# Output projection's first rows read ahead, and attention's first operands loaded during compression

## The chip, the cores and the metric

The kernel runs on one core of a Trainium2 chip. The time is that of the device, in microseconds, from one launch; lower is better. The core has TensorE (matmuls and transposes, into the accumulators of PSUM), VectorE, ScalarE, GpSimd and SyncE, each with an instruction stream of its own; they meet at semaphores. Transfers between memory (HBM) and on-chip tiles go through 16 DMA engines and are issued by SyncE and GpSimd.

## The reference, cut to what matters

One transformer layer for 2048 tokens of width 1024, in float32.

```python
h = rmsnorm(x, g_mix_pre);  z = h @ w_in          # queries, keys, values, gates of 16 heads' worth
o_a = nsa_mixer(...)       # 6 heads: gates * (compressed + selected + window of 512)
o_b = dilated_mixer(...)   # 4 heads, each over three pairs (window, dilation)
o_c = banded_attention(..., sinks=...)            # 6 heads, window of 128
mix = jnp.concatenate([o_a, o_b, o_c], axis=-1) @ w_out
x = x + rmsnorm(mix, g_mix_post)
f = conv_glu_ffn(rmsnorm(x, g_ffn_pre), w_up, conv_w, conv_b, w_down)
x = x + rmsnorm(f, g_ffn_post)
```

Compression turns windows of 32 keys (and values) of the nsa heads into one each: `gelu(flat @ w1 + b1) @ w2`. The compressed attention also chooses the 8 blocks that the selected attention reads.

## The kernel before, in words

Five blocks run one after the other, and a block begins when every engine has finished the one before: `project`, `compress`, `attend`, `mix_out` and `ffn`. Precision is kept by splitting operands into an upper part (rounded) and a lower part (the rest) and using three matmuls.

**project** normalises 16 tiles of 128 rows, turns them, and keeps them on the chip as `h_hi` and `h_lo` (8 rows of blocks c by 2048 tokens). VectorE makes `h_lo` at L410, one operation for each of the 16 tiles. Then 33 blocks of columns of w_in are multiplied (L526) and stored as `z_hi` and `z_lo` in memory. In the last block (L516) the first five rows c are done for all tokens, so that the tiles of rows 0 and 1 come free: SyncE then loads the windows (`x_raw`, over `h_hi`) and first weights (`w1_raw`, over `h_lo`) of the next block into them.

**compress** takes these operands, splits them and multiplies (L650). SyncE issues the second half of the weights, small tables and the overlap table, and waits for the latter.

**attend** has 30 units: a unit is one kind of attention of one head (k: compressed; b: one dilated pair; c: window of 128; w: window of 512; s: selected), of 16 tiles of 128 queries. The order is k, b, b six times, then c six times, then w, s six times. For a tile n TensorE makes scores (L1248, L1249) into one of three PSUM buffers, VectorE adds the bias and finds the lowest (L1437), ScalarE takes the exponential (L1358), TensorE turns the weights (L1260), VectorE or ScalarE copies them (L1344), and once four tiles are turned TensorE multiplies the values (L1285), ScalarE copies the sum (L1366), TensorE turns it back (L1298) and VectorE finishes it (L1461 to L1494). All four engines run one loop over steps n; light tiles have six weight buffers (`w_small`), wide ones three (`w_big`), and scores are issued so many tiles ahead, in the first unit in blocks: tiles 0 to 5 at step 0, 6 to 9 at step 4 (weighed at step 5), 10 to 13 at step 8. Ahead of this loop ScalarE waits for the gates and takes their exponential (L1350), and VectorE prepares the sinks, waits for ScalarE and finishes the gates (L1401 to L1405). TensorE waits ahead of it for the identity matrix. SyncE issues the first loads in this order: identity, queries of unit 0, its table, sinks, gates, queries of unit 1, keys 0, table, values 0, keys 1, values 1. Later loads follow as a unit is scored, biased or summed. The queries lie in `low[:, 0:2]`, the second slot of keys in `low[:, 2:4]`. The last unit of all, the selected attention of head 5, takes its groups of four tiles in falling order (`falling`, `at`), heavy ones first, and uses the wide buffers only. At its end SyncE stores the head and waits for all stores to land.

**mix_out** (the output projection) loads the attention rows of a tile of 128 tokens (L1643 to L1645), turns them (L1809), ScalarE rounds them (L1726) and VectorE makes the lower part (L1763), TensorE multiplies with `w_out` (L1827). The weights were loaded in attention's last units; here ScalarE rounds eight rows of them (L1711), GpSimd and VectorE make the lower parts of four rows each (L1695). VectorE does two of its rows before tile 0's lower part, two after.

**ffn** follows and is not touched but for the place of one scratch tile.

Of the kernel before, what the change touches and what calls it, by code (L numbers as in the profile page):

```python
# [6 lines left out]
F32 = mybir.dt.float32  # L7
F32R = mybir.dt.float32r
# [48 lines left out]
MOVES = tuple(range(6, 22))  # L57

# [14 lines left out]
def project(nc, x, g_pre, ident, w_z, w_ffn, pos_t, z_hi, z_lo, z_pair, v_heads, gates, f_hi, f_lo, w1, w1_copy, w_out, wo_copy, wo_moved,  # L73
# [4 lines left out]
    with ExitStack() as ctx:  # L78
# [5 lines left out]
        idt = sb("idt", [P, P])  # L84
# [83 lines left out]

        def last_of(j):

            return 7 + j if j < 2 else 4 * j + 4

        @blk.sync
        def _(sp):
# [32 lines left out]
            for j in range(2, NZ):  # L207
# [168 lines left out]
        def _(dve):  # L376
# [27 lines left out]
            for t in range(NT):  # L404
                if t >= 6 and t % 2 == 0:
# [4 lines left out]
                dve.tensor_tensor(h_lo[:, :, cols], turned_tile(t % 2), h_hi[:, :, cols].bitcast(F32),  # L410
                                  ALU.subtract).then_inc(hlo_done, 1)
# [36 lines left out]
        def _(pe):  # L448
# [14 lines left out]
            def project_early(i, half):  # L463
# [7 lines left out]
                for c in range(4 * half, 4 * half + 4):  # L471
                    for q, (w, h) in enumerate(((w_hi, h_hi), (w_lo, h_hi), (w_hi, h_lo))):
                        last = pe.matmul(banks[:, bank, :], w[:, j, c, :], h[:, c, tok],
# [31 lines left out]
            for j in range(2, NZ):  # L505
# [4 lines left out]
                for c in range(rows):  # L510
                    for n in range(4):
                        if c == 0:
                            pe.wait_ge(zhi_done, 4 * (j - 2) + n + 1)
                        tok = slice(n * 512, (n + 1) * 512)
                        for q, (w, h) in enumerate(((w_hi, h_hi), (w_lo, h_hi), (w_hi, h_lo))):
                            last = pe.matmul(banks[:, 4 * k + n, :], w[:, k, c, :], h[:, c, tok],  # L516
                                             start=(c == 0 and q == 0), stop=False)
                    last.then_inc(last_row, 1)
                for n in range(4):
# [4 lines left out]
                    for c in range(rows, DC):  # L524
                        for q, (w, h) in enumerate(((w_hi, h_hi), (w_lo, h_hi), (w_hi, h_lo))):
                            last = pe.matmul(banks[:, 4 * k + n, :], w[:, k, c, :], h[:, c, tok],  # L526
                                             start=(c == 0 and q == 0), stop=(c == DC - 1 and q == 2))
# [18 lines left out]
def compress(nc, z_pair, w1_copy, b1_t, w2, overlap, x_raw, w_raw, w_hi, poss, x_in, w_in, pos_in, last_out, kc_hi, kc_lo, vk):  # L546
# [4 lines left out]
    with ExitStack() as ctx:  # L551
# [13 lines left out]
        over_in = sem("over_in")  # L565
        zeroed = sem("zeroed")
# [33 lines left out]
        def _(sp):  # L600
# [5 lines left out]

            sp.wait_ge(zeroed, 3)
# [3 lines left out]
            sp.wait_ge(last_out, 8 * 16)  # L611

        @blk.gpsimd
        def _(pool):
# [10 lines left out]
            pool.memset(vk[0:NC, :, HD:HD + 1], 1.0).then_inc(ones_done, 1)  # L625

# [101 lines left out]
class Unit:  # L728


    def __init__(self, kind, h, fold, back, q_row, k_row, v_head, falling=False):
# [5 lines left out]
        self.at = [4 * (NT // 4 - 1 - t // 4) + t % 4 if falling else t for t in range(NT)]  # L737
        for t in self.at:
# [29 lines left out]
def attention_units():  # L768
# [11 lines left out]
    for h in range(6):  # L780
        units.append(Unit("w", h, 1, 4, h * HD, 13 * P + h // R * HD, 2 + h // R))
        units.append(Unit("s", h, 1, NT - 1, h * HD, 12 * P + h // R * HD, h // R, falling=(h == 5)))
# [30 lines left out]
def attend(nc, ident, z_hi, z_lo, v_heads, gates, bias_b, bias_c, bias_s, bias_w, own_block, sinks, cmp_bias, pick_bias,  # L813
           kc_hi, kc_lo, vk, sel_t, parts, near_parts, o_heads, o_mid, q2, k_hi, k_lo, near, w_small, qm, vs,
           wo_copy, wo_moved, w_rows, w_in):
# [14 lines left out]
    out_at = Slots(heads, lambda u, n: n % 2)  # L830

# [8 lines left out]
    for n in range(N):  # L840
# [6 lines left out]
        mine, size = (narrow, SMALL) if len(unit.tiles[t]) * P <= NARROW and u < NU - 1 else (wide, BIG)  # L847
# [79 lines left out]
    with ExitStack() as ctx:  # L927
        sb, ps, sem = scope(nc, ctx, "a_")
        idt = sb("idt", [P, P])
# [1358 lines left out]
```

## Time and profile before

| | us |
|---|---|
| median of 3 runs | 3513.67 |
| lowest, highest | 3513.1, 3516.63 |
| the profiled execution: its own time | 3511.8 |
| its span, first to last instruction | 3510.0 |
| TensorE busy in it | 3395.0 (97%) |
| VectorE busy | 1387.6 (40%) |
| ScalarE busy | 1161.3 (33%) |
| GpSimd busy | 569.2 (16%) |

In profile rows PE is TensorE's matmuls, PEld its weight loads (beside the matmuls), DVE VectorE, ACT ScalarE, POOL GpSimd, SPq SyncE's queue of issues. "L12" is a line of the kernel. In brackets behind a row stand the idle time of the engine just before and what ended it. The span's mean granted clock of TensorE was 0.989 of full speed. The blocks begin at about 796.5 (compress), 830.7 (attend), 1811.2 (mix_out) and about 2051.2 us (ffn).

### The profile page before, as it was taken

Reading aid. Unit: us, or ns where it says so; the run is one execution under the profiler, and the core shown is the slowest. Engines: PE = TensorE matmul, PEld = TensorE weight load, DVE = VectorE, ACT = ScalarE, POOL = GpSimd, SP = SyncE. Lnnn points to the kernel's source line nnn. Section 1 sums busy time; section 2 is a strip of 40 time slices with the busy share of each in tenths; the row PEclk is TensorE's granted clock in tenths of the full one; section 3 lists DMA queues with packets and bytes.
Section 4 is the critical chain, followed back from the end, with each engine's and each line's share of the span. In section 5 each row is a group of like instructions: output and inputs, shape, how many; then the busy total and the mean of one; then the engine's idle time right before and its main releaser. Section 6 shows DMA issues by size and latency. Waiting matters only on the chain. (4 is left out here: it accounts for less than half of the span.)

```text
span 3510.0 us, 45328 instructions
## 1 busy us (share of the span) xinstructions
PE 3395.0 (97%) x16530; PEld 2708.8 (77%) x16530; DVE 1387.6 (40%) x3825; ACT 1161.3 (33%) x1979; POOL 569.2 (16%) x503
## 2 busy tenths in 40 slices
PE   8999999997998999999989999999999999999998
PEld 6888888886777866666658878887888788888886
DVE  5111101105766766666645444403441244115421
ACT  5111111115665755555433333302330133113310
POOL 1556654430000013232010000000000000000000
PEclk9999999998999999999999999999999999999999
DMA  5789965657888732232036775566556655665553
GB/s 190 265 304 320 320 242 197 213 186 178 205 196 205 174 91 63 77 93 55 28 106 206 234 276 192 192 239 224 192 192 239 232 192 191 239 227 203 191 192 143
DMA packets 299524, 676.15 MB, mean 193 GB/s; under 512 B 99408, under 2 KB 155216, under 8 KB 285136
## 3 DMA queue, kind: packets, MB, share of 16 engines
q1 hardware_dynamic: 265616, 517.93, 45.9%
q0 software_dynamic: 33696, 155.40, 12.3%
q8 instruction: 133, 2.18, 0.3%
q14 instruction: 79, 0.65, 0.1%
HBM read 496.06 MB, written 185.57 MB: 194 GB/s over the span
## 5 line engine op out<-in xcount | busy, mean ns | idle before, releaser
L1285 PE MATMUL a_ot_ps<-a_turned_w,vs 128*65 128x128 f32 (+3 forms) x1452 | 448.6, 420 | 1.2 <-issue 1.2
L526 PE MATMUL z_banks<-h_hi,z_w_hi 128*128 128x512 f32 x972 | 387.3, 398 | 0.0
L526 PE MATMUL z_banks<-h_lo,z_w_hi 128*128 128x512 f32 x972 | 384.5, 396 | 0.0
L526 PE MATMUL z_banks<-h_hi,z_w_lo 128*128 128x512 f32 x972 | 384.4, 395 | 0.0
L1563 PE MATMUL banks<-low,f_own 128*128 128x512 f32 x1344 | 323.7, 401 | 12.4 <-issue 6.3
L1563 PEld LDWEIGHTS banks<-low,f_own 128*128 128x128 f32 x1344 | 258.0, 192 | 73.9 <-issue 13.6
L1358 ACT ACTIVATE w_small<-w_small,a_negm 128x128 f32<-128x128 f32 (+3 forms) x505 | 244.1, 517 | 160.6 <-DVE a_negm L1437 97.1
L1285 PEld LDWEIGHTS a_ot_ps<-a_turned_w,vs 128*65 128x65 f32 x1452 | 179.3, 139 | 81.3 <-issue 68.5
L1437 DVE CUSTOM_DVE_ANT_0 w_small<-a_s_ps,near 128x128 f32<-128x128 f32 (+2 forms) x456 | 169.1, 393 | 168.2 <-PE a_s_ps L1249 141.5
L526 PEld LDWEIGHTS z_banks<-h_lo,z_w_hi 128*128 128x128 f32 x972 | 182.6, 188 | 44.1
L526 PEld LDWEIGHTS z_banks<-h_hi,z_w_lo 128*128 128x128 f32 x972 | 182.8, 188 | 42.7
L526 PEld LDWEIGHTS z_banks<-h_hi,z_w_hi 128*128 128x128 f32 x972 | 182.8, 188 | 42.4
L310 ACT ACTIVATE st_hi<-z_banks 128x512 fp32r<-128x512 f32 (+1 forms) x100 | 59.7, 597 | 462.2 <-PE z_banks L526 331.6
L1260 PE MATMUL a_t_ps<-a_idt,w_small 128*128 128x128 f32 x1077 | 210.0, 277 | 0.0
L445 DVE TENSOR_TENSOR st_lo<-z_banks,st_hi 128x512 fp32r<-128x512 f32 x76 | 52.3, 691 | 396.8 <-ACT st_hi L310 318.0
L1344 ACT ACTIVATE a_turned_w<-a_t_ps 128x512 f32<-128x512 f32 (+3 forms) x255 | 138.7, 548 | 208.0 <-PE a_t_ps L1260 207.1
L2101 DVE SCALAR_TENSOR_TENSOR f_acc<-banks,vk,f_gp 128x1024 f32<-128x1024 f32 x16 | 20.5, 1284 | 454.3 <-POOL vk L1933 454.3
L1248 PE MATMUL a_s_ps<-low 128*128 128x512 f32 (+3 forms) x384 | 186.7, 489 | 2.5 <-DMA low<-z_lo 1.5
L2041 ACT ACTIVATE f_u<-banks 128x512 f32<-128x512 f32 x176 | 105.0, 596 | 237.6 <-PE banks L1563 237.5
L1563 PE MATMUL banks<-low,k_hi 128*128 128x512 f32 x768 | 179.6, 390 | 0.0
L1563 PE MATMUL banks<-low,k_lo 128*128 128x512 f32 x768 | 179.3, 389 | 0.0
L2078 DVE COPY f_u<-f_halo 128x2 f32<-128x2 f32 x176 | 29.7, 169 | 368.7 <-ACT f_u L2041 355.2
(239 smaller groups left out, 6533.2 us busy)
## 6 DMA issues: line engine op xcount, KB each, us to landing
f_own<-f_hi SPq DMA_DIRECT2D x88, 512.0 KB, 3.6
f_own<-f_lo SPq DMA_DIRECT2D x88, 512.0 KB, 4.5
z_xs<-in_w_ffn POOLq DMA_DIRECT2D x33, 1024.0 KB, 8.2
f_hi<-z_v_hi POOLq DMA_DIRECT2D x33, 1024.0 KB, 4.9
f_lo<-z_xs POOLq DMA_DIRECT2D x33, 1024.0 KB, 5.6
low<-z_hi SPq DMA_DIRECT2D x48, 512.0 KB, 7.7
k_hi<-f_hi SPq DMA_DIRECT2D x44, 512.0 KB, 3.6
k_hi<-f_lo SPq DMA_DIRECT2D x44, 512.0 KB, 4.5
```

The lines of the kernel that those rows point to most:

```text
L310: act.activation(out.bitcast(F32) if is_value(j) else out, bank, ACT.Copy).then_inc(zhi_done, 1)
L445: dve.tensor_tensor(low, bank, high, ALU.subtract).then_inc(zlo_done, 1)
L526: last = pe.matmul(banks[:, 4 * k + n, :], w[:, k, c, :], h[:, c, tok], start=(c == 0 and q == 0), stop=(c == DC - 1 and q == 2))
L1248: pe.matmul(out, query, hi[:, start + a:start + z], start=True, stop=False)
L1260: ins = pe.transpose(t_ps[:, b % TB, i, :], weights(n)[:, x * P:(x + 1) * P], idt[:])
L1285: last = pe.matmul(ot_ps[0:out_width(g), at:at + count * P], values, rows, start=(x == 0), stop=(x == len(blocks) - 1), skip_group_check=True)
L1344: ins = eng.activation(out, src, ACT.Copy) if e == 0 else eng.tensor_copy(out, src)
L1358: act.activation(weights(n), weights(n), ACT.Exp, bias=negm[:, n % 32:n % 32 + 1], scale=-1.0)\
L1437: dve.tensor_tensor_reduce(weights(n)[:, a:z], s_ps[:, c % SB, 0:z - a], table[:, at + a:at + z], -0.125, floor, ALU.add, ALU.min, low).th ...
L1563: last = pe.matmul(out, w[:, c * P:(c + 1) * P], rows[:, c, :], start=(c == 0 and x == 0), stop=(c == DC - 1 and x == 2))
L2041: act.activation(u[:, k, b, 2:QT + 2], banks[:, 2 * k + b, :], ACT.Copy).then_inc(u_done, 1)
L2078: dve.tensor_copy(u[:, k, b, 0:2], halo[:, b, j, :]).then_inc(edge_done, 1)
```

## The change

- Compression's SyncE also loads, between its small tables and the overlap table: the queries of units 0 and 1 (`low` rows 0 and 1), the two tables of these units, and the keys of unit 2 (`low` rows 2 and 3). GpSimd's zeroing of the lower half of `low[:, 3]` moves there too. For this `low` and `near` are allocated from the start, and `low` is also the first half of `h_lo` in project, whose other half is the new tile `h_lo2`; the last block's order of rows is `LAST_ROWS`, and the loads of project's end wait for rows 1, 3 and 4 of it.
- Attention's SyncE begins with the keys and values of unit 1 and the values of unit 2, then sinks and gates. TensorE waits for no identity (it stays from project), ScalarE takes the gates' exponential at step 6, VectorE does sinks and gates at the end of step 7.
- The last unit runs in rising order and may use the small buffers. When its first half is finished, SyncE stores that half, and then loads the rows of tiles 0 and 1 of the output projection into the free query slot (`first_o`). The second half's store is no longer waited for in attention (semaphore `o_last`), but in the projection, ahead of the loads of tiles 2 and 3.
- The projection's ScalarE rounds two rows of weights ahead of tile 0, not four, and VectorE makes tile 0's lower part before all its weights.

```diff
+LAST_ROWS = (0, 4, 5, 1, 2, 3, 6, 7)
...
-                    sp.wait_ge(last_row, 2)
+                    sp.wait_ge(last_row, 1)
                     load_windows(sp, z_pair, x_raw, x2_in, 0)
+                    sp.wait_ge(last_row, 3)
                     load_first(sp, w1_copy, w1_raw, w1_in, 0)
+                    sp.wait_ge(last_row, 4)
                     load_windows(sp, z_pair, x_raw, x2_in, 1)
...
-                dve.tensor_tensor(h_lo[:, :, cols], turned_tile(t % 2), h_hi[:, :, cols].bitcast(F32),
-                                  ALU.subtract).then_inc(hlo_done, 1)
+                for part, tile in enumerate(h_lo):
+                    rows = slice(4 * part, 4 * part + 4)
+                    last = dve.tensor_tensor(tile[:, :, cols], turned_tile(t % 2)[:, rows], h_hi[:, rows, cols].bitcast(F32),
+                                             ALU.subtract)
+                last.then_inc(hlo_done, 1)
...
+            first = attention_units()[:3]
+            for s, unit in enumerate(first[:2]):
+                rows = slice(unit.q_row, unit.q_row + HD)
+                sp.dma_start(low[0:HD, s, :].bitcast(F32), z_hi[rows, :]).then_inc(units_in, 16)
+                sp.dma_start(low[HD:P, s, :].bitcast(F32), z_lo[rows, :]).then_inc(units_in, 16)
+            sp.dma_start(near[:, 0, 0:CW], cmp_bias[0]).then_inc(units_in, 16)
+            sp.dma_start(near[:, 1, 0:2 * P], bias_b[0]).then_inc(units_in, 16)
+            rows = slice(first[2].k_row, first[2].k_row + HD)
+            for half in range(2):
+                sp.dma_start(low[half * HD:(half + 1) * HD, 2, :].bitcast(F32), z_hi[rows, :]).then_inc(units_in, 16)
+            sp.dma_start(low[0:HD, 3, :].bitcast(F32), z_lo[rows, :]).then_inc(units_in, 16)
...
+            sp.wait_ge(units_in, 16 * 9)
...
+            pool.memset(low[HD:P, 3, :].bitcast(F32), 0.0).then_inc(ones_done, 1)
...
-        self.at = [4 * (NT // 4 - 1 - t // 4) + t % 4 if falling else t for t in range(NT)]
...
-        mine, size = (narrow, SMALL) if len(unit.tiles[t]) * P <= NARROW and u < NU - 1 else (wide, BIG)
+        mine, size = (narrow, SMALL) if len(unit.tiles[t]) * P <= NARROW else (wide, BIG)
...
+                if u == NU - 1:
+                    sp.dma_start(o_heads[unit.h, :, NT // 2:], oh[:, s, NT // 2:, 0:HD]).then_inc(o_last, 16)
...
-            sp.dma_start(idt[:], ident).then_inc(id_in, 16)
-            load_q(0, 0)
-            load_near(0, 0)
+            load_k(0, 1)
+            load_v(0, 1)
+            load_v(1, 2)
             sp.dma_start(sink[:], sinks.partition_broadcast(P)).then_inc(sink_in, 16)
             sp.dma_start(gate[:], gates).then_inc(gate_in, 16)
-            load_q(1, 1)
-            load_k(0, 1)
-            load_near(1, 1)
-            load_v(0, 1)
-            load_k(1, 2)
-            load_v(1, 2)
+            def load_ahead(u):
+
+                s, h = out_at.slot[out_at.of_unit[u]], units[u].h
+                sp.wait_ge(out_done, 4 * u + 2)
+                sp.dma_start(o_heads[h, :, 0:NT // 2], oh[:, s, 0:NT // 2, 0:HD]).then_inc(stored[s], 16)
+                for e in range(2):
+                    sp.wait_ge(stored[e], out_seen[e])
+                    sp.wait_ge(ob_out[e], 16)
+                sp.wait_ge(scored, through(NU - 3))
+                for t in range(2):
+                    pair = first_o[:, t, :].rearrange("p (h d) -> p h d", d=HD)
+                    sp.dma_start(pair[:, 0:6], heads_in[:, 0:6, t * HD:(t + 1) * HD]).then_inc(ahead_in, 16)
+                    sp.dma_start(first_o[:, t, 384:640], o_mid[t * P:(t + 1) * P, :]).then_inc(ahead_in, 16)
+                    sp.dma_start(pair[:, 10:16], heads_in[:, 6:12, t * HD:(t + 1) * HD]).then_inc(ahead_in, 16)
...
-            for s in range(2):
-                sp.wait_ge(stored[s], out_seen[s])
+            sp.wait_ge(ahead_in, 16 * 6)
...
-            act.wait_ge(gate_in, 16)
-            act.activation(gate[:], gate[:], ACT.Exp, scale=-1.0).then_inc(gexp_done, 1)
-            act.wait_ge(sink_done, 1)
...
             for n in range(N + 6):
+                if n == 6:
+                    act.wait_ge(gate_in, 16)
+                    act.activation(gate[:], gate[:], ACT.Exp, scale=-1.0).then_inc(gexp_done, 1)
...
+                if n == 7:
+                    gates_and_sinks()
...
-            for k in range(2):
-                load_o(k, k)
...
+            sp.wait_ge(o_last, 16)
+            for k in range(2):
+                load_o(2 + k, k)
...
-            for c in range(4):
+            for c in range(2):
                 upper(c)
...
-            split_lower(dve, 1, 0, 4)
             take_o(0, 0)
-            split_lower(dve, 1, 4, DC)
+            split_lower(dve, 1, 0, DC)
...
+                rows = first_o if isinstance(t, int) and t < 2 else ot
```

## Rows read from the trace of the kernel before

**Rows 1.** Waits of TensorE over the span: total us, times, longest

```profile
PE z_banks L459 <- DVE z_xs L391: 16.1, 4, 9.9
...
PE banks L1809 <- DMA p_ot<-o_heads: 11.9, 1, 11.9
PE a_s_ps L1248 <- DMA low<-z_lo: 10.8, 2, 9.2
```

**Rows 2.** Timeline around attention's start: start us, us, engine, line, operation

```profile
829.14 0.29 DVE L724 COPY vk<-c_vc_ps 127x128 f32<-127x128 f32 x1 [0.17 <-PE c_vc_ps L663]
...
830.68 1.28 ACT L1350 ACT_TABLE_LOAD   x1 [2.16 <-PEq L551]
...
838.97 0.44 ACT L1350 ACTIVATE a_gate<-a_gate 128x288 f32<-128x288 f32 x1 [7.00 <-DMA a_gate<-gates]
...
841.77 0.29 DVE L1437 CUSTOM_DVE_ANT_0 w_small<-a_s_ps,near 128x128 f32<-128x128 f32 x1
...
842.17 2.27 ACT L1358 ACTIVATE w_small<-w_small,a_negm 128x128 f32<-128x128 f32 x6 [2.76 <-DVE a_negm L1437]
...
845.01 0.29 DVE L1437 CUSTOM_DVE_ANT_0 w_small<-a_s_ps,near 128x128 f32<-128x128 f32 x1 [1.00 <-PE a_s_ps L1249]
...
845.34 1.68 ACT L1358 ACTIVATE w_small<-w_small,a_negm 128x128 f32<-128x128 f32 x4 [0.17 <-DVE a_negm L1437]
...
848.65 0.28 DVE L1437 CUSTOM_DVE_ANT_0 w_small<-a_s_ps,near 128x128 f32<-128x128 f32 x1
...
851.41 0.29 DVE L1437 CUSTOM_DVE_ANT_0 w_small<-a_s_ps,near 128x128 f32<-128x128 f32 x1
```

**Rows 3.** Timeline of SyncE's issues at attention's start

```profile
833.29 0.43 SPq L1080 DMA_DIRECT2D a_gate<-gates  x1
...
836.18 0.60 SPq L1048 DMA_DIRECT2D k_lo<-z_lo  x1
...
837.45 0.53 SPq L1051 DMA_DIRECT2D vs<-v_heads  x1
```

**Rows 4.** DMA issues of these three moments: count, KB each, us to landing

```profile
a_gate<-gates SPq DMA_DIRECT2D x1, 144.0 KB, 5.7
...
k_lo<-z_lo SPq DMA_DIRECT2D x1, 512.0 KB, 14.9
...
vs<-v_heads SPq DMA_DIRECT2D x1, 520.0 KB, 15.3
```

**Rows 5.** Busy us by engine in compression's later part; then clock, DMA share, GB/s

```profile
808.50:829.00 20.50, 20.50 (x165) 20.05 (x163) 8.62 (x11) 6.79 (x10) 0.00 (x0) 1.00 0.01 2
```

**Rows 6.** The same (PE, PEld, DVE, ACT, POOL) for two stretches of attention's start

```profile
842.10:847.10 5.00, 4.97 (x21) 4.54 (x22) 2.49 (x18) 4.39 (x11) 0.00 (x0) 0.50 1.03 218
848.60:851.40 2.80, 2.43 (x18) 1.85 (x18) 2.20 (x14) 1.61 (x5) 0.00 (x0) 1.00 0.96 231
```

**Rows 7.** Timeline from attention's end into the output projection

```profile
1805.54 0.57 SPq L1074 DMA_DIRECT2D o_heads<-a_oh  x1
...
1815.76 1.94 PE L1809 MATMUL banks<-p_idt,p_ot 128*128 128x128 f32 x8 [11.94 <-DMA p_ot<-o_heads]
...
1821.91 0.78 PE L1827 MATMUL banks<-p_w_hi,p_oh 128*128 128x512 f32 x1
...
1833.86 1.04 PE L1809 MATMUL banks<-p_idt,p_ot 128*128 128x128 f32 x8
```

**Rows 8.** Timeline of VectorE there: first and last of its four weight rows

```profile
1813.22 2.53 DVE L1695 TENSOR_TENSOR p_w_lo<-k_hi,p_w_hi 128x1024 fp32r<-128x1024 f32 x1 [1.93 <-ACT p_w_hi L1711]
...
1823.16 3.42 DVE L1695 TENSOR_TENSOR p_w_lo<-near,p_w_hi 128x1024 fp32r<-128x1024 f32 x1
```

**Rows 9.** Busy us in attention's last two pairs of units, columns as in rows 5

```profile
1619.30:1715.50 96.20, 95.19 (x514) 64.19 (x511) 61.84 (x217) 48.78 (x71) 13.51 (x18) 1.00 0.13 34
1715.50:1803.80 88.30, 85.77 (x453) 56.40 (x450) 51.46 (x170) 41.14 (x56) 4.80 (x7) 1.00 0.15 54
```

**Rows 10.** VectorE's groups by form, first 75 us: count, busy us, mean ns, idle before

```profile
L410 DVE TENSOR_TENSOR h_lo<-z_banks,h_hi 128x1024 fp32r<-128x1024 f32 x16 | 19.5, 1221 | 9.1 <-ACT h_hi L281 9.1
```

More of the change, by code:

```diff
@@ L167, in early @@
             return 4 + i % 4, i % 4, i % 2, i // 2
+        hi_rows, lo_rows = [h_hi[:, c] for c in range(DC)], [h_lo[c // 4][:, c % 4] for c in range(DC)]
         def last_of(j):
@@ L509, in _ @@
                 rows = 5 if j == NZ - 1 else 0
-                for c in range(rows):
+                order = LAST_ROWS if rows else tuple(range(DC))
+                for c in order[:rows]:
                     for n in range(4):
-                        if c == 0:
+                        if c == order[0]:
                             pe.wait_ge(zhi_done, 4 * (j - 2) + n + 1)
                         tok = slice(n * 512, (n + 1) * 512)
-                        for q, (w, h) in enumerate(((w_hi, h_hi), (w_lo, h_hi), (w_hi, h_lo))):
-                            last = pe.matmul(banks[:, 4 * k + n, :], w[:, k, c, :], h[:, c, tok],
-                                             start=(c == 0 and q == 0), stop=False)
+                        for q, (w, h) in enumerate(((w_hi, hi_rows), (w_lo, hi_rows), (w_hi, lo_rows))):
+                            last = pe.matmul(banks[:, 4 * k + n, :], w[:, k, c, :], h[c][:, tok],
+                                             start=(c == order[0] and q == 0), stop=False)
                     last.then_inc(last_row, 1)
@@ L523, in _ @@
                     tok = slice(n * 512, (n + 1) * 512)
[L524 to L527, printed above, removed]
+                    for c in order[rows:]:
+                        for q, (w, h) in enumerate(((w_hi, hi_rows), (w_lo, hi_rows), (w_hi, lo_rows))):
+                            last = pe.matmul(banks[:, 4 * k + n, :], w[:, k, c, :], h[c][:, tok],
+                                             start=(c == order[0] and q == 0), stop=(c == DC - 1 and q == 2))
                     last.then_inc(z_done, 1)
@@ L543, with compress @@
 PICKED = 2e30
-def compress(nc, z_pair, w1_copy, b1_t, w2, overlap, x_raw, w_raw, w_hi, poss, x_in, w_in, pos_in, last_out, kc_hi, kc_lo, vk):
+def compress(nc, z_pair, w1_copy, b1_t, w2, overlap, x_raw, w_raw, w_hi, poss, x_in, w_in, pos_in, last_out, kc_hi, kc_lo, vk,
+             z_hi, z_lo, bias_b, cmp_bias, low, near):
     U = T // 2
@@ L1734, in _ @@
             take_o(0, 0)
-            for c in range(4, DC):
+            for c in range(2, DC):
                 upper(c)
@@ L1808, in turn_o @@
                 for c in range(DC):
-                    last = pe.transpose(t1[:, c, :], ot[:, k, c * P:(c + 1) * P], idt[:])
+                    last = pe.transpose(t1[:, c, :], rows[:, k, c * P:(c + 1) * P], idt[:])
                 last.then_inc(o_turned, 1)
@@ L2185, in layer @@
     with ExitStack() as keep:
+        idt = keep.enter_context(nc.sbuf_tensor("idt", [P, P], F32))
+        near = keep.enter_context(nc.sbuf_tensor("near", [P, 2, NARROW], F32))
+        low = keep.enter_context(nc.sbuf_tensor("low", [P, 4, T], F32R))
         kc_hi = keep.enter_context(nc.sbuf_tensor("kc_hi", [P, G, P], F32R))
```

110 lines of the change are left out of this document (55 added, 55 removed).

## The prediction, made before the change was run

> **What bounds the kernel now.** I read the busy times first, on the page's first part: TensorE works for nearly the whole span, the next engine for 40% of it. So time can only come out of what still makes TensorE wait, or out of stretches in which its clock is low. The list of its waits comes next [rows 1]. The change touches three of them: 11.9 us at the start of the output projection, for the attention output read back from memory; 10.8 us in attention for queries (9.2 at its start, the rest at its third unit); and 16.1 us in the first stage, behind VectorE. Then I read the timeline around the two places where a stage begins, and the times to landing of the transfers there.
>
> **Attention's start, before.** Compression's last instruction ends at 829.4 and attention's first starts at 830.7 [rows 2]: 1.2 us to pass from one block to the next. The first score matmul stands 9.2 us for the queries [rows 1], until 838.3. Even that doesn't set the pace: VectorE and ScalarE work on the gates first. ScalarE's exponential of the gates runs at 838.97, VectorE's two operations follow it, and the first bias of a score comes at 841.77 [rows 2], 2.80 us after the exponential. From there ScalarE weighs tiles 0 to 5 (842.17) and 6 to 9 (from 845.34, 1.68 us, to 847.0); tiles 10 to 13 get their bias from 848.65 on.
>
> **What moves there.** The nine new loads in compression are seven of 512 KB and two tables. Price of one load: between the landing of the gates (833.29 + 5.7 = 839.0) and that of the lower half of the first keys (836.18 + 14.9 = 851.1) five loads of 512 KB land [rows 3, 4], 2.42 us each. The values that land next do so at 837.45 + 15.3 = 852.8, 1.7 us later for themselves and a small table; I take 1.45 us for the values and 0.2 for the table. So the nine need 7 x 2.42 + 2 x 0.2 = 17.3 us. In compression the DMA engines are idle from 808.5 on (share 0.01) [rows 5]: done at about 826, 3.4 us before the block ends. They cost nothing under that cover, and every microsecond beyond 829.4 would be a microsecond of the total. The small transfer of the overlap table is now queued behind them and lands with them. GpSimd's clearing of half of a key tile moves along, to an engine with nothing after it.
>
> First bias is then possible at 830.7 + 0.7 = 831.4, but the table load of ScalarE (1.28 us from 830.68 [rows 2]), hidden before, ends at 832.0; first exponential 832.0 for 842.17: **10.2 us earlier**.
>
> **What becomes late next.** SyncE's order changes too: the first pair's keys (three loads) and two loads of values now go out before sinks and gates. The gates land where they did, less idt, two query loads and the table (0.3 + 4.84 + 0.2), plus three key loads and two of values (7.26 + 2.9): 839.0 - 5.3 + 10.2 = **843.8**. ScalarE asks for them at its step 6, right after weighing tile 9, which it reaches 847.0 - 842.2 = 4.9 us after its first exponential, at 836.9. There it stands, for 7 us. Queued behind it: taking the first group's output, and tiles 10 on; VectorE waits for the exponential of the gates before it goes on to the bias of tiles 10 to 13, and TensorE for VectorE, with the fourth of these scores, since three score buffers are full. Bias of tile 10: 843.8 + 2.80 = 846.6, for 848.65: of the 10.2 us **2.05 are left**.
>
> Next, the clock. Before, it fell during the wait for the queries: from 842.1 to 847.1 TensorE works again, busy and granted half (1.2 GHz), and has the full 2.4 GHz from 848.6 to 851.4 [rows 6]. After the change it is idle from about 838 to 846.6, nearly as long as then, so I expect it at 1.2 GHz for as long again, while tiles 10 to 17 are done. Mostly at the low clock four tiles took 848.65 - 845.01 = 3.64 us, at the full one 851.41 - 848.65 = 2.76 [rows 2]: 0.9 us for four tiles, two such groups: **1.8 us lost**. The Trainium skill (TensorE: Matmul & The Clock Gate, section Why this matters for your kernels) asks to leave no idle gap between bursts of matmuls, or the array returns to half rate; the trace agrees, and by that rule moving the gap speaks against the change as much as having it.
>
> The third unit's queries: they go out when unit 0 is scored (after 851.4) and found a queue full of keys and values; TensorE waited 10.8 - 9.2 = 1.6 us for them [rows 1]. Now the queue has run empty before they go out: **1.6 us gained**, and I add **0.9** for VectorE's waits for tables in the same full stretch (bound: 0 to 2). Sum at this place: 2.05 - 1.8 + 1.6 + 0.9 = **2.7 us gained**. Bounds: 0 (the low clock lasts twice as long and the third unit's wait was slack), and 13 (rival A).
>
> **The output projection, before.** The last head's store goes out at 1805.54; SyncE waits for it to land, the block changes, the first rows are loaded (TensorE waits 11.9 us for them [rows 1]) and turned at 1815.76, ScalarE and VectorE split them, and the first projection matmul is at 1821.91 [rows 7].
>
> **After.** SyncE no longer waits for the last store: it ends at 1805.54 + 0.57, and with 1.2 us for the change of block the projection begins at 1807.3. Rows of tiles 0 and 1 lie in a query tile that is free, and the identity stays where it was: TensorE turns them at once, 1815.76 - 1807.3 = **8.4 us earlier**. The chain behind is as before, 1821.91 - 1815.76 = 6.15 us: ScalarE now rounds two rows of weights ahead of it in place of four (2.0 us, beside the 1.94 us of turning). First matmul 1813.5. One new order: VectorE splits weights only after it has split tile 0, from 1811.8; its four rows took 2.5 us, 2.5, 3.4 and 3.4 (the first and the last: [rows 8]), so the last is ready at 1811.8 + 11.9 = 1823.7. TensorE's first tile took 1833.86 - 1821.91 = 11.95 us for eight rows of weights [rows 7]; it wants the eighth after 7/8 of that, at 1824.0. It fits by 0.3 us; bound: 1 us lost. TensorE's clock is low here both times (it was idle before both).
> The six loads of these rows go out behind a wait for the first half of the last head, some 25 us before the end, when DMA is near idle (share 0.15 [rows 9]); nothing on SyncE stands behind them but waits for later events. The loads of tiles 2 and 3 wait for the last store, but are wanted only at about 1825.
>
> **Rising order in the last unit.** For the early half store the last chosen unit runs from light tiles to heavy ones, and may use the small buffers. TensorE's work is the same. It is idle for 88.30 - 85.77 = 2.5 us of the last pair of units, and the pair before, rising, for 1.0 us in 96.2 [rows 9]. The end now drains heavy tiles, with less beside them. I take **0**; bounds 1.5 gained (the difference of the two) and 2.5 lost (the idle doubled).
>
> **First stage.** h_lo is two tiles, so VectorE subtracts twice 512 columns in place of once 1024. 1024 take 1.221 us [rows 10] and 128 (of another operation) 0.29 [rows 2], so some 0.16 us of each operation is fixed: that much more for each tile. It lies on the path for the first four tiles only, where TensorE waits for VectorE [rows 1]; 0.5 us lost. Later TensorE is full there. Rows 0, 4, 5, 1 of the last block's order free the tiles of x and weights at about the same times: the windows go out 2.5 us earlier, the first weights 0.3 later, the second windows 2.4 later, all behind TensorE, before the stores at 788. Nothing.
>
> **Sum.** 8.4 + 2.7 + 0 - 0.5 = 10.6 us. Against the profiled execution (3511.8 us): 3501.2. The median of the three shown, 3513.67, lies 1.9 above it, so a median would be about 3503.
>
> **Rivals.**
> A. The gates are in time, or ScalarE gets to them later than I count. For it: only that they are a small transfer, 144 KB. Against it: on this queue each landed after all that was issued before it [rows 3, 4]. Then 10.2 stay, 1.8 comes back for the clock that doesn't fall, 0.7 is lost for keys that land at 839.9, 1.6 for the third unit: 13 at this place, 20.9 in all, 3493. The Trainium skill (DMA: Bandwidth & Descriptors, Queues, rings and completion order) says that completion isn't first in, first out for one issuing engine; no row here shows one that overtook.
> B. Attention's start gives nothing (longer low clock, the third unit's wait was slack) and the drain of heavy tiles costs 1 to 2.5: 8.4 - 0.5 - 2 = 5.9, 3508. For it: VectorE is busy 2.20 us of 2.80 at that place [rows 6], so what one wait returns another may take.
> C. Slower: the nine loads outlast compression. Past 829.4 each microsecond counts once; it decides when they end later than 829.4 + 10.6 = 840, so 31.5 us for what I price at 17.3. At 4.84 us a load (double) they end at 843, for 3517. Against it: 2.42 us was measured beside a busy TensorE, and here the queue is empty.
>
> **Numbers.** Forecast 0.65, A 0.13, B 0.18, C 0.04. The forecast's own range is 3500 to 3506. The range: from A (3492) to B (3508). A measurement of this kernel can't tell less than 0.2% (7 us) from no change. Faster: 0.93 of the forecast, all of A, 0.4 of B: 0.80. Within: the rest of these, 0.16. Slower: C, 0.04.
>
> **What would show it.** The first score matmul within 1 us of attention's start; ScalarE standing some 7 us before L1350's exponential of the gates, gates landing at about 844; the granted clock at half until 850; no wait for queries at the third unit; compression's length unchanged at 829.4; the projection's first matmul 6.2 us after its first turn, and that within 2 us of the last store. Wrong, if ScalarE doesn't stand there, if the compression block is longer, or if the last unit takes over 2 us more.

## The result, and the profile after

The changed kernel takes 3519.13 us (median of 17 runs, 3516.11 to 3524.18), beside 3513.38 us for the kernel before on the same chips (17 runs, 3507.21 to 3517.76). The ratio is 1.0018, with a 95% interval of 1.0011 to 1.0025: slower by 0.18%. The forecast was 3503, with a range of 3492 to 3508. Its profiled execution took 3518.79 us, of which 3516.93 are the span.

Cut at instants that both traces have, the two executions divide like this (us; the instants are those of the timelines, the differences are taken from them):

| stretch | before | after | difference | forecast |
|---|---|---|---|---|
| first stage, to compression's first instruction | 796.53 | 793.01 | -3.5 | +0.5 |
| compression, to attention's first instruction | 34.14 | 33.30 | -0.8 | 0 |
| attention, to the issue of the last head's store | 974.87 | 971.99 | -2.9 | -2.7 |
| from there to the projection's first matmul | 16.37 | 9.46 | -6.9 | -8.4 |
| projection, to the feed-forward's first load | 229.49 | 232.18 | +2.7 | 0 |
| feed-forward | 1458.58 | 1476.99 | **+18.4** | 0 |
| span | 3509.98 | 3516.93 | +6.9 | -10.6 |

So the changed kernel reaches its feed-forward 11.5 us earlier, for 10.6 forecast (4.3 of it in two stretches that were to gain nothing), and then loses 18.4 in a stage that the diff doesn't reorder. First that stage, by windows: length, busy time of TensorE with its count of matmuls, granted clock, DMA share, GB/s. Before:

```profile
2051.40:3509.98 1458.58, 1434.98 (x6240) 0.99 0.56 208
```

After:

```profile
2039.94:3516.93 1476.99, 1453.40 (x6240) 0.99 0.55 206
```

Equal counts, equal clock, nearly equal DMA share, and the same idle time (23.6 us both times). TensorE doesn't wait longer; it is busy 18.4 us longer with as many matmuls. The group of the page that shows it, before:

```profile
L1563 PE MATMUL banks<-low,k_hi 128*128 128x512 f32 x768 | 179.6, 390 | 0.0
```

and after (with the waits of TensorE under it, the counterpart of [rows 1]):

```profile
L1599 PE MATMUL banks<-low,k_hi 128*128 128x512 f32 x768 | 184.4, 396 | 0.0
```

```profile
PE a_s_ps L1281 <- DVE a_negm L1471: 24.3, 26, 7.1
PE z_banks L466 <- DVE z_xs L395: 16.3, 4, 9.9
...
PE banks L1843 <- PEq L952: 5.3, 1, 5.3
PE banks L1843 <- DVE p_ol L1797: 2.4, 1, 2.4
```

390 ns became 396 for each matmul of the up phase on the ring's tiles k_hi, k_lo, qm and vs (the up phase multiplies with w_up, the down phase with w_down; the ring is the set of tiles into which their weights are loaded in turn, and f_own holds its last two places). Ends of matmuls are modelled, so the pace is better taken from start to start: 626.1 us for the 2760 such steps that both traces recorded before, 644.1 after, that is 226.8 and 233.4 ns. These steps alone lose 18.1 us, nearly the whole loss. On f_own the step went from 232.4 to 233.3, and in the down phase nothing moved (its four parts take 496.4 and 496.3 us). In the waits, the two that the change was about are gone (11.9 us for p_ot, 10.8 for low), a wait of 7.1 us behind VectorE and one of 5.3 at the change of block have come.

Attention's start, the counterpart of [rows 2, 3]:

```profile
826.35 0.30 PE L1281 MATMUL a_s_ps<-kc_hi,low 128*128 128x128 f32 x1 [1.56 <-PEq L560]
...
826.80 0.29 DVE L1471 CUSTOM_DVE_ANT_0 w_small<-a_s_ps,near 128x128 f32<-128x128 f32 x1 [1.60 <-PE a_s_ps L1282]
...
827.61 1.86 ACT L1387 ACTIVATE w_small<-w_small,a_negm 128x128 f32<-128x128 f32 x6
...
829.98 0.43 SPq L1106 DMA_DIRECT2D a_gate<-gates  x1
...
830.22 1.68 ACT L1387 ACTIVATE w_small<-w_small,a_negm 128x128 f32<-128x128 f32 x4 [0.17 <-DVE a_negm L1471]
...
838.55 0.17 DVE L1434 TENSOR_SCALAR a_nsink<-a_sink 128x6 f32<-128x6 f32 x1 [4.22 <-DMA a_sink<-in_sinks]
838.73 0.44 ACT L1413 ACTIVATE a_gate<-a_gate 128x288 f32<-128x288 f32 x1 [6.83 <-DMA a_gate<-gates]
...
839.55 1.95 DVE L1438 RECIPROCAL a_gate<-a_gate 128x288 f32<-128x288 f32 x1
841.54 0.29 DVE L1471 CUSTOM_DVE_ANT_0 w_small<-a_s_ps,near 128x128 f32<-128x128 f32 x1
```

The first score comes 0.04 us after attention's start, and ScalarE stands 6.83 us for the gates, which are ready at 838.73. The bias of tile 10 comes 15.2 us after attention's start; before it was 18.0. The windows of TensorE there:

```profile
826.31:829.31 3.00, 2.93 (x17) 0.85 0.67 172
829.31:832.31 3.00, 3.00 (x13) 0.50 1.02 216
...
835.30:838.30 3.00, 0.00 (x0) 0.50 0.91 339
...
841.30:844.30 3.00, 2.41 (x9) 0.50 0.01 3
844.30:847.30 3.00, 2.94 (x19) 0.81 0.00 0
```

The granted clock falls in the first, at 828.4, while TensorE works: it had been idle for 1.56 us at the change of block, and has 2 us of work behind it. At 835.3 it has been at the lower level (1.2 GHz, granted 0.50) for 7 us, and only then comes the idle stretch. The full level is back within the last window, at 845.5. Before, TensorE was idle from 829.1 and the clock fell at 833.5, inside the wait for the queries, and was back at 847.2.

The change of block, and the projection's start, the counterpart of [rows 7]:

```profile
1798.30 0.38 SPq L1092 DMA_DIRECT2D o_heads<-a_oh  x1
1801.80 0.34 SPq L1680 DMA_DIRECT2D p_gp<-in_g_mix_post  x1
...
1801.83 1.94 PE L1843 MATMUL banks<-idt,low 128*128 128x128 f32 x8 [5.26 <-PEq L952]
...
1807.76 0.78 PE L1861 MATMUL banks<-p_w_hi,p_oh 128*128 128x512 f32 x1
```

### The profile page after: what moved, and what is told of

Read it like the earlier page. It is cut to its first block and busy times, and to the rows that moved or that the text cites. A ratio compares the mean times of both kernels' runs of the same rounds, so it can differ in the third digit from the quotient of the medians.

```text
span 3516.9 us, 45339 instructions
## 1 busy us (share of the span) xinstructions
PE 3413.2 (97%) x16530; PEld 2707.3 (77%) x16530; DVE 1388.1 (39%) x3841; ACT 1160.7 (33%) x1979; POOL 569.7 (16%) x503
## 3 DMA queue, kind: packets, MB, share of 16 engines
q0 software_dynamic: 33696, 155.40, 12.3%
## 5 line engine op out<-in xcount | busy, mean ns | idle before, releaser
L1318 PE MATMUL a_ot_ps<-a_turned_w,vs 128*65 128x256 f32 (+3 forms) x1452 | 449.4, 421 | 1.1 <-issue 1.1
L1599 PE MATMUL banks<-low,f_own 128*128 128x512 f32 x1344 | 323.9, 400 | 12.5 <-issue 6.3
L1599 PEld LDWEIGHTS banks<-low,f_own 128*128 128x128 f32 x1344 | 256.3, 191 | 76.0 <-issue 13.7
L1293 PE MATMUL a_t_ps<-idt,w_small 128*128 128x128 f32 x1092 | 212.5, 278 | 0.0
L534 PE MATMUL z_banks<-h_lo,z_w_hi 128*128 128x512 f32 x488 | 191.8, 393 | 0.0
L534 PE MATMUL z_banks<-low,z_w_hi 128*128 128x512 f32 x484 | 190.3, 393 | 0.0
L1599 PE MATMUL banks<-low,k_hi 128*128 128x512 f32 x768 | 184.4, 396 | 0.0
L1599 PE MATMUL banks<-low,k_lo 128*128 128x512 f32 x768 | 184.4, 396 | 0.0
```

The source lines that it names most:

```text
L534: last = pe.matmul(banks[:, 4 * k + n, :], w[:, k, c, :], h[c][:, tok], start=(c == order[0] and q == 0), stop=(c == DC - 1 and q == 2))
L1293: ins = pe.transpose(t_ps[:, b % TB, i, :], weights(n)[:, x * P:(x + 1) * P], idt[:])
L1318: last = pe.matmul(ot_ps[0:out_width(g), at:at + count * P], values, rows, start=(x == 0), stop=(x == len(blocks) - 1), skip_group_check=True)
L1599: last = pe.matmul(out, w[:, c * P:(c + 1) * P], rows[:, c, :], start=(c == 0 and x == 0), stop=(c == DC - 1 and x == 2))
```

## The experiments

**The theories.** The change adds no work to the feed-forward, but it moves tiles. It keeps the identity and the tables (idt, near) and low in front of everything else, so the tiles start at other bytes of a partition's memory. In the kernel before, low begins at byte 19360 and k0_hi, the ring's first tile, at 52128: 32 x 1024 apart. After, they are at 22144 and 57760, 32 x 1024 + 2848 apart, since kc_hi, kc_lo and vk (2848 bytes), once in front of low, now lie between low and the ring. That is 32 modulo 256. low holds the moving rows of every up matmul, the ring's tiles the stationary blocks. Theory P: TensorE's pace depends on this distance. Rival Q: something beside TensorE (DMA, the other engines), or how the instructions lie, slows it.

**1. map: TensorE alone.** One line of the kernel for each placement, 73 in all (the expectation says 105). M is where the moving rows start, R how far behind them, modulo 1024, the stationary blocks start. The body of a line, shortened:

```python
last = [pe.matmul(banks[:, r, :], big[:, (at(M) + far + R + w * 4096 + c * 512) // 4:][:, :P],
                  big[:, (at(M) + h * 16384 + c * 2048) // 4:][:, :512], ...)
        for r in range(4) for c in range(8) for w, h in ((0, 0), (1, 0), (0, 1))][-1]
```

> This kernel computes none of the reference: TensorE alone runs the 24 matmuls of one up step (three products for each of eight rows, 128x512 float32r), four times over for each of 105 placements, one source line each: the moving rows start at M bytes modulo 1024 in a partition and the stationary blocks M + R later. Nothing else runs beside it. Theory P (the pace depends on where the two operands lie in a partition): the lines with R = 0 at M = 928, the placement of the kernel before, run at about 227 ns from start to start, and those with R = 800 (the placement of the changed kernel) at about 233; the 32 steps of R show which distances are fast, and the 16 steps of M whether the distance alone or the absolute place counts. Theory Q (the pace differs because of something that runs beside TensorE, or because of the instructions' own layout): all lines lie within 1 ns of each other.

The chain of this kernel, one row per placement: start, us for its 96 matmuls, line. L37 to L45 are M = 928 and R = 0, 32, 64 to 256, L53 is R = 512, L69 and L85 are M = 0 with R = 0 and R = 800 (32 modulo 256, as in the changed kernel):

```profile
71.18 21.77 PE banks L37 x96
92.95 22.39 PE banks L38 x96
115.34 22.40 PE banks L39 x96
137.74 22.48 PE banks L40 x96
160.22 22.30 PE banks L41 x96
182.53 22.40 PE banks L42 x96
204.93 21.99 PE banks L43 x96
226.91 22.39 PE banks L44 x96
249.31 21.77 PE banks L45 x96
...
427.44 21.77 PE banks L53 x96
...
783.69 21.81 PE banks L69 x96
...
1132.52 22.40 PE banks L85 x96
```

21.77 / 96 is 226.8 ns a matmul, 22.39 to 22.48 are 233.2 to 234.2. The row repeats with R every 256 bytes: 226.7 at 0, 233.3 at 32 and 64, 234.2 at 96, 232.3 at 128, 233.4 at 160, 229.0 at 192, 233.3 at 224. Sixteen values of M, 64 bytes apart, give 227.1 each at R = 0 and 233.3 each at R = 800: the distance counts, the place hardly (227.1 for 226.8 at M = 928). Both paces of the two kernels come out of it with nothing running beside TensorE. So do both of f_own: before, it lies 128 off low modulo 256, for which the map says 232.3 and the kernel showed 232.4; after, it lies 160 off, 233.4 and 233.3. Q falls.

**2. after_rel0: the changed kernel with 224 empty bytes.**

```diff
+        keep.enter_context(nc.sbuf_tensor("gap56", [P, 56], F32))
         k0_hi = keep.enter_context(nc.sbuf_tensor("k0_hi", [P, T], F32R))
```

> The changed kernel with 224 bytes left empty between the h tile (low) and the ring of weights, so that their distance is again a multiple of 1024, as it was before. Theory P: the up phase goes back from 233.3 to about 227 ns a matmul, 18 us in all; 3501 us, faster than both kernels (ratio to the kernel before 0.997). Theory Q: the up phase stays at 233 and the time at 3519.

Measured: 3500.43 us (6 runs) beside 3514.21 (9), ratio 0.9965, interval 0.9953 to 0.9978. The group of L1599 and the window of the feed-forward:

```profile
L1599 PE MATMUL banks<-low,k_hi 128*128 128x512 f32 x768 | 179.6, 389 | 0.0
```

```profile
2039.35:3497.26 1457.91, 1434.36 (x6240) 0.99 0.57 208
```

The pace (390 ns there) and the 1458 us of the kernel before are back. 224 bytes of nothing turn a kernel that is 0.18% slower into one that is 0.35% faster.

**3. before_rel288 and before_both288: the same from the other side.** The first has 288 empty bytes between low and k0_hi of the kernel before, the second has them ahead of low, so that both move.

> The kernel before with 288 bytes left empty between low and the ring; nothing else of the change. Theory P: the up phase's matmuls on the ring go from 226.8 to some 233 ns; 3531 us, 18 us slower than the kernel before. Theory Q: 3513, unchanged.

> The kernel before with 288 bytes left empty ahead of low, so that low and the ring move together: their distance stays a multiple of 1024, their own places change. If only the distance counts: 227 ns a matmul in the up phase and 3513 us. If the absolute place of either counts: some 233 ns and about 3531 us.

before_rel288: 3532.64 us (4 runs), ratio 1.0049, interval 1.0032 to 1.0066. Its feed-forward:

```profile
2055.90:3531.40 1475.50, 1452.62 (x6240) 0.99 0.57 206
```

That is 16.9 us more than before, at 233.3 ns a matmul: nearly the loss of the changed kernel, in a kernel without the change. before_both288: 3517.41 us in its one run, with 226.7 to 227.0 ns a matmul on the ring. The pace says that the distance counts and not the place, as the map does. Its time is 3.2 us above the median of the kernel before, whose own runs beside it went from 3507.8 to 3517.2; one run can't tell whether that is more than chance.

**4. map2: the operands shifted one by one.**

> As map, TensorE alone and none of the reference computed, but the third product's moving rows (h_lo) lie D bytes (0 to 224 in steps of 32) off the place of the first two's (h_hi), for each distance R of 0 to 224 between stationary and moving; and at R = 0 the second product's stationary block (w_lo) is shifted instead. Theory A (each matmul's own two operands must match): D and R add for one product in three, so R = 0 with any D not 0 gives 226.7 + (233.3 - 226.7) / 3 = 228.9. Theory B (the moving rows being read conflict with the next matmul's stationary block being loaded): as A in size, but R = 0 with D costs in the third product's step and R not 0 with D = R gains there, and the first stage's mix (R = 32 and 64 modulo 256) gives some 230.5, as was measured.

D is how many bytes further off the third product's moving rows (h_lo) start than those of the first two (h_hi). Here the sizes of both theories fail. With the first two products at distance 0 and only the third's moving rows D bytes off, the pace is 231.7, 231.9, 231.1, 233.2, 232.3, 229.3 and 231.0 for D = 32 to 224, mostly far above the 228.9 of theory A; shifting only w_lo gives 231.1 to 233.3. Theory B wants a gain at D = R: there is one at 96, 128, 160 and 224 (at 128 228.9 for 233.3), none at 32 and 64, and at 192 a loss (231.1 for 229.0). With R = 32 throughout, D = 224 gives 231.2 where D = 0 gives 233.4. So a matmul's own two operands aren't all that counts; which pair of accesses it is stays open. One thing can be read off for use: of the 64 combinations of R and D, all at 0 is the fastest (226.7), and none comes nearer to it than 228.9.

It bears on the first stage too. There the weights lay 32 from h_hi and from h_lo, modulo 256 (233.3 in the map, 233.3 in the trace). In the changed kernel low is the first half of h_lo and lies 224 off h_hi: 231.2 in map2 (R = 32, D = 224). By that, half of the 33 blocks x 96 matmuls should gain 2.1 ns each, 3.3 us, and the stage became 3.5 shorter. But the trace divides it otherwise: the mean step is 232.2 ns where low is read and 232.5 where the other half, h_lo2, is read, whose distances didn't change. 1.0 ns on 3168 matmuls is about 3 us. So the size fits placement, and why h_lo2's half gains as well is open. (The 230.5 that the expectation calls the stage's pace is that of the third product alone.)

**5. aligned: every operand at the same remainder.** The kernel is the changed one. The gap of run 2 moved ahead of h_hi, 224 bytes more ahead of w_raw, 128 ahead of own and of g_hi, and the projection's eps behind its large tiles:

```diff
+        sb("gap32a", [P, 32])
         own = sb("own", [P, RING - AHEAD, 2, D], F32R)
...
+        sb("gap32b", [P, 32])
         g_hi = sb("g_hi", [P, NF, QT], F32R)
```

> The changed kernel with every tile that a 128x512 float32r matmul of the first stage, the output projection or the feed-forward reads placed at the same remainder modulo 256 bytes: the 224 empty bytes of after_rel0 moved ahead of h_hi, and 224 more ahead of the first stage's weights, 128 ahead of f_own, 128 ahead of g_hi, and the projection's small eps tile moved behind its large ones. Theory P, by the pace per matmul in the map (226.7 at a distance of 0 modulo 256, 232 to 234 elsewhere): first stage about 3300 matmuls x 5.8 ns = 19 us less than after_rel0, up phase on f_own 1400 x 6 = 8.5, down phase on f_own some 5, output projection 768 x 6.6 = 5; together 37 us less than after_rel0's 3500: 3463. If the first stage is held by something else than TensorE's pace (VectorE and ScalarE follow it), only some 18 us come: 3482.

Measured: 3466.21 us (4 runs) beside 3513.64, ratio 0.9864, interval 0.9848 to 0.9881; a second time 3464.78, ratio 0.9865 (0.985 to 0.988).

> The kernel of the run aligned, for comparison on the same chip: 3466.

Against after_rel0 the first stage is 15.9 us shorter in the profile (19 expected), the projection 4.2 (5), the feed-forward 12.3 (13.5). The steps are now 226.6 to 227.7 ns in all three stages. Theory P holds in each, and TensorE's pace bounds the first stage too.

**6. before_aligned: the change by itself.** The same placement in the kernel before.

> The kernel before with the placement of the run aligned (everything that a 128x512 float32r matmul reads at one remainder modulo 256) and none of the change. Theory P plus the prediction's sum: with placement taken out on both sides, the change itself gives the 10.6 us forecast, so this kernel is 10.6 us slower than aligned: 3477 for aligned's 3466. If the extra 3 us seen between the kernel before and after_rel0 (13.8 in place of 10.6) were the change's own and not the first stage's placement, it would be 14 us slower than aligned: 3480.

Measured: 3474.25 us (4 runs, 3471.44 to 3476.31), beside 3464.78 for aligned on the same chip (4 runs, 3464.48 to 3467.45): the change itself is worth 9.5 us by the medians. Forecast were 10.6. In the two profiles it is 11.4: first stage 0.2, compression 0.5, attention 4.2, from the last head's store to the projection's first matmul 7.0, projection 0.0, feed-forward 0.4 lost. With placement equal on both sides the prediction's sum stands; the 14 us that after_rel0 seemed to show held 3.5 of the first stage, most of it placement.

**7. rel0_gates: sinks and gates first.**

```diff
-            load_k(0, 1)
-            load_v(0, 1)
-            load_v(1, 2)
             sp.dma_start(sink[:], sinks.partition_broadcast(P)).then_inc(sink_in, 16)
             sp.dma_start(gate[:], gates).then_inc(gate_in, 16)
+            load_k(0, 1)
+            load_v(0, 1)
+            load_v(1, 2)
```

> after_rel0 with sinks and gates loaded ahead of the first pair's keys and values at attention's start, nothing else. Theory G (ScalarE's wait for the gates is what keeps most of the attention start's gain away): ScalarE's stall of 6.8 us ahead of the gates' exponential is gone, TensorE's clock doesn't fall there, and the time is 7 to 10 us below after_rel0's 3500.4: 3491 to 3493. Rival: the keys of the second unit, now landing some 2 us later, or the third unit's queries become the wait: ScalarE's stall goes and TensorE's comes, less than 3 us gained.

Measured: 3493.80 us (4 runs), ratio 0.9944 (0.9926 to 0.9961), so 6.6 below after_rel0 by medians, with intervals that overlap a little. In the profile attention is 3.5 us shorter. Its timeline:

```profile
833.15 0.43 ACT L1413 ACTIVATE a_gate<-a_gate 128x288 f32<-128x288 f32 x1
...
835.99 1.95 DVE L1438 RECIPROCAL a_gate<-a_gate 128x288 f32<-128x288 f32 x1
...
837.98 0.29 DVE L1471 CUSTOM_DVE_ANT_0 w_small<-a_s_ps,near 128x128 f32<-128x128 f32 x1
```

and TensorE's windows, from attention's start at 827.65:

```profile
827.65:830.65 3.00, 2.94 (x17) 0.92 0.47 97
830.65:833.65 3.00, 3.00 (x13) 0.50 1.07 254
836.65:839.65 3.00, 1.32 (x7) 0.50 0.96 313
```

ScalarE's stall is gone, no wait for keys takes its place, and the bias of tile 10 comes 10.3 us after attention's start in place of 15.3. But only 5 of the 6.9 us come: VectorE now first takes out a tile and then spends 1.95 on the gates' reciprocal, with the same scores queued behind it. And the clock is at the lower level all the same, from 2.5 us after the start, though TensorE is working without a pause when it falls (830.1; the full level is back at 843.8). Theory G was right on the wait, wrong on the clock, and too large on the worth: 7 to 10 us, where the profile shows 3.5 and the medians, from different chips, 6.6.

**8. rel0_wait: the wait that the change took away, put back.**

> after_rel0 with SyncE waiting again for the last head's store before attention's block ends. Theory D (SyncE's drain at the end of the block takes some 1.5 us after a transfer has just been issued, so that most of the store's landing is waited for anyway): the output projection's block starts 4.1 us after that store's issue in place of 3.5, 0.6 us later. Rival (the drain has nothing to do with the store): 1.6 us after the landing as well, but the drain stays at 1.5 us on top of it, 5.6 us after the issue.

```profile
1799.83 0.38 SPq L1092 DMA_DIRECT2D o_heads<-a_oh  x1
1804.02 0.34 SPq L1681 DMA_DIRECT2D p_gp<-in_g_mix_post  x1
```

4.19 us from the store's issue to the next block's first in place of 3.50, as theory D expected. But the time fits another cause as well, and the small records of SyncE and GpSimd (start us, engine, record; for GpSimd's drain its length) speak for the other one:

```
changed kernel   1797.70 POOL DRAIN 2.73   1798.30 SP DMA_DIRECT2D   1798.91 SP DRAIN   1800.47 POOL EVENT_SEMAPHORE
rel0_wait        1799.22 POOL DRAIN 2.72   1799.83 SP DMA_DIRECT2D   1802.66 SP DRAIN   1802.69 POOL EVENT_SEMAPHORE
before           1804.94 POOL DRAIN 2.72   1805.54 SP DMA_DIRECT2D   1809.80 SP DRAIN   1809.83 POOL EVENT_SEMAPHORE
```

The block ends with GpSimd's EVENT_SEMAPHORE record, which waits for the other engines. GpSimd itself gets there only after its own drain, which begins 0.2 us after the start of its last addition of attention (L1221) and takes 2.72 to 2.73 us in every run. SyncE's drain takes 0.007 us. In the changed kernel GpSimd's drain ends at 1800.42 and the record follows 0.04 us later; in after_rel0 they are at 1801.13 and 1801.18, in aligned at 1784.62 and 1784.67. In rel0_wait and in the kernel before it has ended (at 1801.94 and 1807.66) when SyncE arrives, and is hidden. So theory D's reason, SyncE's drain, isn't borne out: what is left when the wait for the store goes is GpSimd's drain. No run takes GpSimd's last addition away, which would be the direct test.

**9. aligned_gates: the best of both.**

> The kernel of aligned with sinks and gates loaded first at attention's start, as in rel0_gates. Attention was 3.5 us shorter there in the profile and the medians differed by 6.6: 3460 to 3463, faster than both kernels (ratio to the kernel before 0.985). If the two edits don't add up: 3466.

Measured: 3458.15 us (5 runs, 3456.33 to 3460.97) beside 3512.11 (9 runs), ratio 0.9846, interval 0.9832 to 0.9859: 1.5% faster than the kernel before and 1.7% faster than the changed one (on other chips). It is 6.6 us below aligned_again, and 2 below the range expected. The edits add up.

## Why the prediction was wrong, and where it was right

**The feed-forward: the step that failed.** The change part by part has no term for the feed-forward, and none for where tiles lie. The diff moves idt, near and low to the front, and the sum puts that at nothing without a reason. It costs 18.4 us, more than all that the change gains: each matmul on the ring steps every 233.4 ns in place of 226.8. Nothing of it shows as a wait; in the profile before it could have been suspected from two groups of the page that differ in nothing but their tile, low with k_hi at 390 ns and low with f_own at 401. Experiments 1 to 3 show it. Which accesses of TensorE collide stays open (experiment 4).

**The sum.** 10.6 us were forecast, 9.5 are measured between two kernels of equal placement, and after_rel0, the changed kernel with the old distance, stands at 3500.4 for the 3503 forecast. That sum is partly luck: terms that were too large and too small make up for each other, as follows.

**Attention's start: the wait right, the sum partly luck.** ScalarE's stall was forecast as 7 us, it is 6.83; the gates at 843.8 on the clock of the trace before, they came 12.4 us after attention's start, which is 843.1 there. The bias of tile 10 was to gain 2.05 and gains 2.75; the clock was to cost 1.8, and by tile 14 the gain is down to 1.0. The third unit's queries were to give 1.6 back and gave 1.75: from then on it is 2.8. The 0.9 for VectorE's waits for tables didn't come there. 2.75 were forecast for this place, with 0.7 too little in one term and 0.9 too much in another.

The reason given for the clock failed, though not its price. The prediction has it fall in the wait for the gates; it fell at 828.4, 7 us ahead of that wait, and in rel0_gates it fell without the wait. The Trainium skill (TensorE: Matmul & The Clock Gate, section Why this matters for your kernels) ties the lower level to idle gaps. The wait of the kernel before agrees (idle from 829.1, lower level from 833.5). That the changed kernel and rel0_gates were granted half speed 2 to 2.5 us into unbroken work is nothing that a gap inside attention explains; ahead of it lay the 1.6 us of the change of block. No run here settles what made it fall.

**The end of attention and the rising order.** Attention as a whole gained 2.9. The gain stood at 3.65 before the last unit, and that unit in rising order costs some 0.8 us of it. That is inside the bounds of -1.5 to 2.5; that the total is so near to the 2.7 forecast is chance.

**The projection's start: 6.9 for 8.4.** The missing 1.5 is the term "1.2 us for the change of block", taken from the end of compression, where VectorE's last copy ends the block and GpSimd has nothing left to do. Here GpSimd's drain of 2.72 us begins 0.6 us ahead of the store's issue (experiment 8), and the block begins 3.5 us after that issue where 1.8 were forecast. The drain is in the trace before as well, until 1807.66. Of the 6.9 us, 4.6 are the rows that no longer need loading, 0.7 the removed wait, and 1.4 the store's size: half a head, 256 KB, lands in 2.5 us where 512 KB took 4.0. The last 0.2 is the chain behind. From the first turn to the first matmul 6.15 was forecast, 5.93 it is.

**The projection itself: 2.7 lost for 0.** The bound was 1 us. The eighth row of weights was there in time, but the first tile took 12.95 us for 11.95. TensorE's granted clock over its first 4 us, before:

```profile
1821.90:1826.00 4.10, 4.10 (x17) 0.82 1.08 294
```

and after:

```profile
1807.80:1812.00 4.20, 4.20 (x13) 0.57 1.19 299
```

The other 1.7 us lie in no one place (0.7 at tile 10 in this execution, and not in after_rel0, where the stage is 1.3 shorter). That the weights' new order is free isn't shown by this. In aligned_again the full clock is back 1.5 us into the stage, and there TensorE catches up with the splitting: 7.6 us into it a step takes 703 ns in place of 227. The prediction's bound is real, and in the changed kernel the lower level hides it. In before_aligned the lower level reaches 4.3 us into the stage, which then takes the same 226.3 us as in aligned_again.

**Compression: right.** The nine loads have landed by 819.9, 6 us before the block ends, and cost nothing; the block is 0.8 us shorter. Rival C is out. **The first stage: wrong in sign**, 3.5 gained for 0.5 lost; some 3 us of it are TensorE's faster steps (experiment 4).

**The rivals.** A is out by the landing of the gates, B by attention's start. The loss came from none of the four cases, and the slower side had a chance of 0.04.

## What to carry over

When a change adds, removes or reorders tiles, print where every large tile starts, before and after, and compare the distances modulo 256 bytes between the tiles that one matmul reads; a stage that the diff doesn't touch can lose more than the change gains. In the profile, look for matmul groups of one shape whose mean differs by their tile: here that was placement, and a few empty bytes mended it. Before a wait at a block's end is taken away, look at what every other engine still has to finish there: here GpSimd's drain took its place.

## What the runs showed of the hardware that was not expected

- 128x512 float32r matmuls, in this kernel's order of three products, step every 226.7 ns when all stationary blocks and moving rows start a multiple of 256 bytes apart, and every 229.0 to 234.2 when the stationary blocks are off by other multiples of 32 (230.0 to 233.3 at 4 to 24 bytes), with TensorE alone and at 0.99 of its clock. The Trainium skill (TensorE: Matmul & The Clock Gate, section Step-by-step: what each phase is for) gives 216 ns for 512 columns at the full clock and a throughput of purely the number of columns. No row here shows 216 for this type, and the 3% between placements are outside that rule; the measurement decides.
- Over the whole kernel this is worth 38 us in the kernel before (3474.25 for 3512.11, experiment 6), 1.1%, for 480 empty bytes in a partition and one small tile moved.
- GpSimd's drain at the end of attention, behind an addition of 128x256 (0.68 us), takes 2.72 to 2.73 us in every run; without the wait for the store the block's end follows it by 0.04 us. SyncE's drain takes 0.007 us right after an issue.
- The granted clock fell to half 2.1 us (changed kernel) and 2.5 us (rel0_gates) into attention, with TensorE busy for 2.93 and 2.94 of the first 3 us.
